# Softmax attention of two stages rebuilt: probabilities divided on GpSimd, values stationary, output born turned

## The reference

```python
# first block, for each head: the selected and the window branch
# (512 tokens: all blocks are selected and the window holds all, so both are causal softmax attention)
p_s = masked_softmax(q @ k_slc.T * scale + bias, causal)
p_w = masked_softmax(q @ k_win.T * scale + bias, causal)
y_a = (g0 * o_c + g1 * (p_s @ v_slc) + g2 * (p_w @ v_win)) @ w_up_nsa
mixed = (sigmoid(m_a) * y_a + sigmoid(m_b) * y_b) @ w_out
# second block: own and past key blocks together, causal
h_a = softmax(q_a @ k_a.T * scale, causal) @ v_a
mix = concatenate([h_m, h_a], axis=-1) @ w_out_2
```

## Time and profile before

| | us |
|---|---|
| median of 3 runs (1792.4 to 1796.67) | 1793.6 |
| span of the profiled execution (first to last instruction) | 1789.7 |
| sw, first score to the closing dummy matmuls | 284.4 to 373.0 |
| stick_breaking begins; mix_branches begins | 376.3; 457.7 |
| ma, first score to the closing dummy matmuls | 1165.0 to 1210.4 |
| out_route begins | 1212.6 |
| busy, share of the span: PE, PEld, DVE, ACT, POOL | 94%, 64%, 43%, 28%, 11% |

### The profile page before, as it was taken

The page is one execution under the profiler, slowest core; times in us unless marked ns, Lnnn a source line. Parts: engine busy times, 40 slices in busy tenths (PEclk is TensorE's granted clock), DMA queues, the critical chain, the costliest instruction groups (busy, mean ns, idle before and its releaser), DMA issues. The chain is left out here.

```text
span 1789.7 us, 21660 instructions
## 1 busy us (share of the span) xinstructions
PE 1676.2 (94%) x8246; PEld 1148.9 (64%) x8247; DVE 776.4 (43%) x1339; ACT 500.7 (28%) x821; POOL 190.5 (11%) x250
## 2 busy tenths in 40 slices
PE   6999999999999999999999999989999999999982
PEld 4788887766777878878887778778833333333321
DVE  7345224768676688423335455454621111111114
ACT  4322324546323212222224433253211011111101
POOL 1020000000112122200003000001211011110101
PEclk9999999989999999999999999999999999999996
DMA  9423220025444677422221222127799999999995
GB/s 309 116 71 118 94 94 1 1 78 180 173 153 164 215 239 246 151 71 94 94 94 36 89 76 71 48 98 300 314 378 424 423 424 424 425 424 425 424 418 210
DMA packets 114500, 366.34 MB, mean 205 GB/s; under 512 B 21723, under 2 KB 24967, under 8 KB 89807
## 3 DMA queue, kind: packets, MB, share of 16 engines
q1 hardware_dynamic: 108219, 355.45, 52.7%
q0 software_dynamic: 5760, 9.02, 1.4%
q10 hardware_dynamic: 404, 0.30, 0.1%
HBM read 359.85 MB, written 16.84 MB: 210 GB/s over the span
## 5 line engine op out<-in xcount | busy, mean ns | idle before, releaser
L2505 PE MATMUL x_upa<-x_ring,x_Ta 128*64 128x512 f32 x608 | 135.1, 593 | 12.1 <-DMA x_ring<-in_w_expert_up_dram 12.1
L2505 PE MATMUL x_gpa<-x_ring,x_Ta 128*64 128x512 f32 x608 | 135.8, 599 | 4.8 <-DMA x_ring<-in_w_expert_gate_dram 3.1
L2505 PEld LDWEIGHTS x_upa<-x_ring,x_Ta 128*64 128x64 f32 x608 | 46.6, 137 | 97.9 <-issue 97.9
L2505 PEld LDWEIGHTS x_gpa<-x_ring,x_Ta 128*64 128x64 f32 x608 | 46.2, 138 | 90.7 <-issue 88.8
L374 DVE TENSOR_TENSOR p_lo<-p_raw,p_hi 128x2048 fp32r<-128x2048 f32 (+1 forms) x20 | 44.8, 2238 | 137.0 <-ACT p_hi L687 137.0
L381 PE MATMUL fr_p<-p_hi,u_high 128*128 128x512 f32 x224 | 89.1, 398 | 0.0
L382 PE MATMUL fr_p<-p_lo,u_high 128*128 128x512 f32 x224 | 88.0, 393 | 0.0
L383 PE MATMUL fr_p<-p_hi,u_low 128*128 128x512 f32 x224 | 88.0, 393 | 0.0
L2567 ACT ACTIVATE x_siga<-x_gpa 128x512 f32<-128x512 f32 x19 | 11.3, 597 | 241.6 <-PE x_gpa L2505 241.6
L2530 PE MATMUL x_y0a<-x_ring,x_aTa 128*64 128x512 f32 x304 | 72.9, 600 | 5.1 <-ACT x_aTa L2572 4.5
L687 ACT ACTIVATE p_hi<-p_raw 128x2048 fp32r<-128x2048 f32 (+1 forms) x20 | 37.4, 1872 | 125.0 <-DMA p_raw<-in_w_in_dram 125.0
(11 more groups left out here) (886 smaller groups left out, 3979.9 us busy)
## 6 DMA issues: line engine op xcount, KB each, us to landing
x_ring<-in_w_expert_up_dram SPq DMA_DIRECT2D x64, 1024.0 KB, 28.1
x_ring<-in_w_expert_down_dram SPq DMA_DIRECT2D x64, 1024.0 KB, 27.7
x_ring<-in_w_expert_gate_dram SPq DMA_DIRECT2D x64, 1024.0 KB, 26.9
p_raw<-in_w_in_dram SPq DMA_DIRECT2D x18, 1024.0 KB, 5.1
adaw0m<-in_w_ada_dram SPq DMA_DIRECT2D x6, 2048.0 KB
adaw1m<-in_w_ada_dram SPq DMA_DIRECT2D x6, 2048.0 KB, 9.2
ada_first<-in_ada_w_dram SPq DMA_DIRECT2D x8, 1024.0 KB, 5.3
w_raw0m<-in_mlp_w_dram SPq DMA_DIRECT2D x8, 1024.0 KB, 7.2
```

The source lines that it names most:

```text
L2505: mm = nc.tensor.matmul(ps[CAP * f:CAP * f + CAP, :], self.xT[:, k, CAP * f:CAP * f + CAP], w[m + f][k // 4][:, k % 4, :], start=(k == 0), ...
```

## The change

`HeadPairs` goes, and `softmax_attention` is written anew.

- DVE inverts the sums after three tiles and again after the fourth (`invert`), and POOL multiplies each tile's probabilities in SBUF by that coefficient, and in sw by the gate too, before they are turned: 8 instructions a pair.
- `pT` now holds a whole head (four key blocks of 512 queries) and there are two, one for each head. ACT copies the second head's turned tiles, all four, and DVE the first head's. In ma they lie in the space of `heads_out`.
- `weigh` runs once a pair: the values (128x64) are stationary, the turned probabilities move (512, 384, 256 and 128 columns for key blocks 0 to 3), and the two heads go to partitions 0 to 63 and 64 to 127 of one bank. In sw the second branch accumulates on the first in PSUM, and 8 more matmuls against the identity add `B.oa`, the compressed branch.
- One DVE instruction a unit (`take`) copies the bank out, in sw with a negative step that undoes the reversed order. The output has its columns on the partitions, so the flips of `mix_branches` and half of the transposes of `out_route`, with their copies, go. The rows of `w_up_nsa` are loaded in the new order of the heads by two DMAs of 64 partitions.
- PE's list: the scores of the next pair are split around the turning of tile 3 of the first head.

```diff
+    def __init__(self, keys, values, gate=None):
+        self.keys, self.values, self.gate = keys, values, gate
...
+TURN_BANK = [0, 0, 1, 0]
+TURN_COL = [0, P, 0, 0]
...
+def softmax_attention(nc, C, tag, qT, branches, out, units=4, bias=None, shared_out=None, flipped=False, turned_at=None, ahead=None, after=None):
...
+        def turned_of(j):
+            return tps[TURN_BANK[j]][:, TURN_COL[j]:TURN_COL[j] + P * (j + 1)]
+        def copy(eng, op, p, h, j):
+            eng.wait_ge(turned, 8 * p + 4 * h + max(j, 1) + 1)
             if j == 0:
+                eng.wait_ge(weighed, p)
+            op(pT[h][:, 0:j + 1, P * j:P * j + P], turned_of(j).rearrange("p (b n) -> p b n", n=P)).then_inc(copied[h], 1)
         with nc.Block() as block:
             @block.sync
             def _(sp):
@@ -1367,80 +1283,139 @@
 
             @block.tensor
             def _(pe):
+                def scores(p, order):
+                    i, br = p // nb, branches[p % nb]
+                    for h, j in order:
+                        r = slice(64 * h, 64 * h + 64)
+                        if (h, j) == (1, 1):
+                            pe.wait_ge(shared, p + 1)
+                        mm = nc.tensor.matmul(logits_of(h, j), qT(i)[r, P * j:P * j + P], br.keys(i, h, P * (j + 1))[r, :],
+                                              start=True, stop=True)
+                        if (h, j) == (0, 1):
+                            mm.then_inc(shared, 1)
+                    if order[-1] == PAIR_ORDER[-1]:
+                        mm.then_inc(scores_ready, 1)
+                def turn(p, h, j):
+                    pe.wait_ge(scaled, 8 * p + 4 * h + j + 1)
+                    if j == 0:
+                        pe.wait_ge(copied[1 - h], 4 * (p + h))
+                    elif j == 3:
+                        pe.wait_ge(copied[h], 4 * p + 2)
+                    for b in range(j + 1):
+                        mm = nc.tensor.transpose(turned_of(j)[:, P * b:P * b + P], probs_of(h, j)[:, P * b:P * b + P], C.ident[:, :])
+                    mm.then_inc(turned, 1)
+                def weigh(p):
+                    i, k = p // nb, p % nb
+                    last = k == nb - 1
+                    for h in range(2):
+                        pe.wait_ge(copied[h], 4 * p + 4)
+                    if k == 0:
+                        pe.wait_ge(out_done, i)
+                    for b in range(NT):
+                        for h in range(2):
+                            mm = nc.tensor.matmul(ops[64 * h:64 * h + 64, P * b:TOK], branches[k].values(b, h, i), pT[h][:, b, P * b:TOK],
+                                                  start=(k == 0 and b == 0), stop=(last and not shared_out and b == NT - 1),
+                                                  skip_group_check=True)
+                    if last and shared_out:
+                        for j in range(NT):
+                            for h in range(2):
+                                mm = nc.tensor.matmul(ops[64 * h:64 * h + 64, P * j:P * j + P], shared_out(j, h, i), C.ident[:, :],
+                                                      start=False, stop=(j == NT - 1), skip_group_check=True)
+                    mm.then_inc(weighed, 1)
+                scores(0, PAIR_ORDER)
+                fill(nc, C, ops, 3)
+                for p in range(pairs):
+                    for j in range(3):
+                        turn(p, 0, j)
+                    if p + 1 < pairs:
+                        pe.wait_ge(scores_read, 8 * (p + 1))
+                        scores(p + 1, PAIR_ORDER[:4])
+                    turn(p, 0, 3)
+                    if p + 1 < pairs:
+                        scores(p + 1, PAIR_ORDER[4:])
+                    for j in range(NT):
+                        turn(p, 1, j)
+                    weigh(p)
+                fill(nc, C, sps[0], 2)
...
+                def logits(p, h, j):
                     if j == 0:
+                        if h == 0:
+                            dve.wait_ge(scores_ready, p + 1)
+                        if p:
+                            dve.wait_ge(turned, 8 * p - 4 + 4 * h)
+                    v.tensor_tensor_reduce(probs_of(h, j), logits_of(h, j), (bias(h, p // nb) if bias else C.ban)[:, P * (NT - 1 - j):512],
+                                           1.0, 3e38, ALU.add, ALU.min, low[h][:, j:j + 1]).then_inc(scores_read, 1)
+                def invert(p, h, a, b):
+                    dve.wait_ge(exps, 8 * p + 4 * h + b)
+                    v.reciprocal(coef[h][:, a:b], sums[h][:, a:b]).then_inc(coef_ready, 1)
+                def take(i):
+                    dve.wait_ge(weighed, nb * (i + 1))
+                    x = ops[:, :]
+                    if flipped:
+                        x = bass.AP(tensor=x.tensor, offset=x.offset + P - 1, ap=[x.ap[0], [P, NT], [-1, P]])
+                        v.tensor_copy(out(i).rearrange("p (t n) -> p t n", n=P), x).then_inc(out_done, 1)
+                    else:
+                        v.tensor_copy(out(i), x).then_inc(out_done, 1)
                 if bias:
                     dve.wait_ge(C.bias_in, 16)
+                for p in range(pairs):
+                    for j in range(NT):
+                        logits(p, 0, j)
+                    logits(p, 1, 0)
+                    logits(p, 1, 1)
+                    invert(p, 0, 0, 3)
+                    logits(p, 1, 2)
+                    invert(p, 0, 3, NT)
+                    logits(p, 1, 3)
+                    invert(p, 1, 0, 3)
+                    for j in range(3):
+                        copy(dve, v.tensor_copy, p, 0, j)
+                    invert(p, 1, 3, NT)
+                    copy(dve, v.tensor_copy, p, 0, 3)
+                    if p and p % nb == 0:
+                        take(p // nb - 1)
+                take(units - 1)
...
+            @block.gpsimd
+            def _(pool):
+                for p in range(pairs):
+                    gate = branches[p % nb].gate
+                    for h in range(2):
+                        for j in range(NT):
+                            pool.wait_ge(coef_ready, 4 * p + 2 * h + 1 + (j == 3))
+                            if gate:
+                                ins = pool.tensor_scalar(probs_of(h, j), probs_of(h, j), coef[h][:, j:j + 1], gate(h, p // nb)[:, j:j + 1],
+                                                         ALU.mult, ALU.mult)
+                            else:
+                                ins = pool.tensor_scalar(probs_of(h, j), probs_of(h, j), coef[h][:, j:j + 1], None, ALU.mult)
+                            ins.then_inc(scaled, 1)
...
+                def copies(p):
                     for j in range(NT):
+                        copy(act, lambda dst, src: nc.scalar.activation(dst, src, ACT.Copy), p, 1, j)
+                for p in range(pairs):
+                    if p:
+                        copies(p - 1)
+                    for h in range(2):
+                        for j in range(NT):
+                            act.wait_ge(scores_read, 8 * p + 4 * h + j + 1)
+                            nc.scalar.activation(probs_of(h, j), probs_of(h, j), ACT.Exp, scale=-1.0, bias=low[h][:, j:j + 1],
+                                                 accum_out=sums[h][:, j:j + 1]).then_inc(exps, 1)
+                copies(pairs - 1)
...
-                for k in range(4):
-                    for t in range(NT):
-                        mm = nc.tensor.matmul(tps[k][:, P * t:P * t + P], B.oa[:, t, P * k:P * k + P], C.flip[:, :],
-                                              start=True, stop=True)
-                    mm.then_inc(turned, 1)
...
-                    low(v, low_of[0][0][:, k, :], tps[k][:, :], high[0][0][:, k, :]).then_inc(heads_low, 1)
+                    low(v, low_of[0][0][:, k, :], B.oT[0][:, k, :], high[0][0][:, k, :]).then_inc(heads_low, 1)
...
-                    act.wait_ge(turned, k + 1)
-                    copy(high[0][0][:, k, :], tps[k][:, :], heads_high)
-                act.wait_ge(w_in[0], 16)
+                    copy(high[0][0][:, k, :], B.oT[0][:, k, :], heads_high)
+                act.wait_ge(w_in[0], 32)
...
+        own_heads = 4
...
-                for k in range(KD):
+                for k in range(own_heads):
                     for t in range(NT):
                         mm = nc.tensor.transpose(ps[k][:, P * t:P * t + P], cat(t, k), C.ident[:, :])
                     mm.then_inc(turned, 1)
...
-                        for b, n in enumerate(("w_up_nsa", "w_up_sb")):
-                            sp.dma_start(wu[b][:, :, :], A[n][0].rearrange("(k p) n -> p k n", p=P)).then_inc(w_in[b], 16)
+                        for half in range(2):
+                            sp.dma_start(wu[0][64 * half:64 * half + 64, :, :],
+                                         A["w_up_nsa"][0, 256 * half:256 * half + 256, :].rearrange("(k d) n -> d k n", d=HD)).then_inc(w_in[0], 16)
```

(12 more changed lines are left out.)

234 lines of the change are left out of this document (42 added, 192 removed).

## The result

Nine runs of the changed kernel on the chip have a median of 1807.46 us (1803.98 to 1811.18), nine of the kernel before 1795.86. The ratio is 1.0065, 95% interval 1.0048 to 1.0082: slower by 11.6 us, where 1780.5 and a gain were forecast. The profiled execution spans 1808.9 us. The stages, from first matmul to first matmul, read from the timeline, in brackets the time with TensorE at half clock. Mixing counts from its first product, so the 16 flips stand in the row of stick_breaking where there are any.

The account below looks back on a forecast made before the run. PE and its short waits were taken to bound sw and ma, 134.0 us. New pairs of 9.35 us gave 79.6 + 41.3 = 120.9, a gain of 13.1: 1776.6 profiled, plus 3.9 makes 1780.5 us; range 1770 to 1801.

Parts of the forecast that it names:

- S: POOL's scaling of a whole pair's eight tiles: 5.6 us, between 4.8 by select and 6.4 by two inputs.
- The second rival: POOL becomes the bound, deciding from S = 7.2 on; with S = 7.8 the kernel takes 1801 us; chance 0.11.
- The long ring: Chain through ACT, DVE, POOL and PE from one pair to the next: 7.45 us plus POOL's three tiles, 9.15.
- steps 1 to 11: The long ring's parts in order, from three exponentials to ACT's copy of 512 columns: 9.15 us in all.
- steps 5 and 7: The next pair's first four scores, 1.53 us; DVE's copy of 512, 0.74, with the other four scores, 0.83, beside it.
- step 4: Hand-over and PE's turning of three blocks of tile 2 on the long ring: 0.38 us.
- step 9: ACT's copies of 128 and 256 columns of the second head, with hand-over, on the long ring: 0.6 us.
- T: Time of one pair in sw and ma: 9.35 us, the long ring's 9.15 plus 0.2 for matmul mode changes.
- The third rival: TensorE's clock falls in both stages; at half clock for half the time, 15 us slower, 1809; chance 0.12.
- 8T + 4.8: Length of sw, its pairs plus the stage's ends: 79.6 us.
- 4T + 3.9: Length of ma, its pairs plus the ends, with -1.5 for the last pair's missing four scores: 41.3 us.
- the ring through POOL: Shorter ring in both stages, through POOL's whole pair: 3.04 + S, 8.6 us a pair.

Follow-up runs that it names:

- the first experiment: The changed kernel with a second scalar, a column of ones, in POOL's scaling instruction in ma: 1794.02 us, ratio 0.9984.
- 3: The changed kernel with the gate left out of sw's scaling, so that POOL's instruction there has one scalar too: 1825.66 us in one run.
- 8: The changed kernel with 14 POOL instructions of 128x512 in different scalar forms added behind ma's last pair: 1817.71 us in one run.
- the fifth experiment: The fourth experiment's kernel with the compressed branch's records ahead of the second branch's weighing and the bank's copy behind the next pair's last logits: 1792.53 us, ratio 0.9975.
- the fourth experiment: The first experiment's kernel with dummy matmuls of 128 columns in PE's waits: 1793.61 us, ratio 0.9971.
- 10: The ninth's kernel with the next pair's first four scores reordered, PE waiting for the eighth logits only ahead of the fourth score: 1787.18 us, ratio 0.9947.
- 11: The kernel of 10 with the next pair's last two scores moved behind the second head's turning of tile 2: 1787.17 us, ratio 0.9961.
- the ninth: The fifth experiment's kernel with DVE scaling only tile 2 of the first head and POOL the other seven tiles: 1786.79 us, ratio 0.9947.
- 6: The fifth experiment's kernel with DVE scaling the first head's first three tiles and POOL the other five: 1791.14 us, ratio 0.9967.
- experiment 12: The changed kernel with the fourth experiment's dummy matmuls, POOL's one-scalar form left in ma: 1805.82 us, ratio 1.0043.
- experiment 7: The kernel before, run unchanged for a second profile: 1793.08 us in one run.

## Why the prediction was wrong

**The step that failed** is POOL's price: "The new instruction has one tensor and one or two scalars from memory, so I take the middle of select and two inputs: S = 5.6". One value was taken for two forms. sw's is at the lower bound (4.75), ma's above the upper one (8.5 for 7.8), and I had let the count of inputs speak for the price. The second rival gave the mechanism, S above 7.2, and its formula holds: 3.04 + 8.5 = 11.54 for pairs of 11.62. Its time, 1801, was for both stages at 7.8. Experiments 1, 3 and 8 show the price from three sides. The first takes 8.1 us out of ma, 5.4 of it by the distance of its pairs, 9.82 in place of 11.62 three times.

The profile's span is 32.3 us over the 1776.6 forecast. ma is 13.0 over its 41.3 (8.1 the price, 2.4 the clock, the rest the steps below), sw 7.4 over its 79.6, the mixing stage 0.2, `out_route` 1.4, and some 10 lie in code that is as before.

- *The long ring in sw.* POOL's three tiles took 1.67 with the hand-over, as taken. The round shown is 0.68 over the 9.15 of steps 1 to 11. The two pieces of scores (steps 5 and 7) make 0.4 of it: eight in a row took 2.36, in two pieces they take 1.71 + 1.06 = 2.77. The sum had 0.2 for all changes between half and full rows. "TensorEngine Tiling", Key Properties, in the Trainium skill, by which each change drains the array, would have had 0.2 more and was nearer; the two pieces, 0.2 us each over their share of the unbroken run, agree with it in kind. Tile 2's turning (step 4) and ACT's first copies (step 9) were 0.1 each over. At the seam of two units `B.oa` and the bank's copy make the pair 10.16 where 9.69 stands between; T was 9.95 on the mean where 9.35 was forecast. On the ring itself that is 10.02 and 9.82, as the fifth experiment shows.
- *Weighing* takes 2.2 us as worked out, so the halves run together.
- *The clock.* The third rival had 0.50 for half of the time of both stages; it was 21 of 141 us. It struck the last pair of either stage, 2.3 us in sw and 2.4 in ma by the fourth experiment; an earlier fall in ma (1198.4 to 1201.9) left its pair at 11.62. The last weighing of ma takes 4.07 us where 2.2 was forecast:

```profile
1222.13 1.09 PE L1318 MATMUL opsma<-pT0ma,va 128*64 128x512 f32 x1 [0.73 <-issue]
...
1226.20 1.98 PE L147 MATMUL sps0ma<-ban,ident 128*128 128x512 f32 x4
```

- *The stage's ends.* 8T + 4.8 gives 84.4 for T = 9.95, and 2.3 of clock 86.7, for 87.0 measured. In ma 4T + 3.9 gives 50.4 for T = 11.62, and 54.3 were measured. The clock's 2.4 are part of that, and the -1.5 for step 5 doesn't belong there: the ring through POOL has no step 5 to leave out.
- *Mixing stage and out_route.* Right: from SP's first instruction of the mixing stage to the next stage's first matmul it was 64.0 us and is 64.2; the first product of `out_route` comes 3.7 behind its start for 3.8. In place of flips and transposes PE waits:

```profile
460.83 0.53 PE L381 MATMUL mx<-wu_high,oT_high 128*128 128x512 f32 x1 [3.04 <-DVE oT_low L374]
```

```profile
1232.24 0.47 PE L381 MATMUL dp0o<-w_hi0o,ah0o 128*128 128x512 f32 x1 [1.82 <-DVE al0o L2176]
```

- *"All later stages start by as much earlier"* took their length for fixed. Of the 19.2 us between the two spans ma, sw and mixing account for 7.7 (9.0 - 1.5 + 0.2) and `out_route` for 1.4, with 3 us more at half clock; 10.1 lie in code that is as before. The medians are 11.6 apart, 7.7 of it shown by those three stages. Runs of the kernel before differ in the granted clock too, 0.985 in one of 1792.84 us and 0.977 in one of 1800.25; its median was 0.980, 0.972 for the changed kernel, 0.978 for experiments 1, 4 and 5. Why the unchanged stages of the changed kernels tend to more time at half clock (`out_route` 10 us in place of 7 in most, 7 in experiments 10 and 11, which then took 84.0) stays open: no run tells a shift of the stages in time from chance.

Had the price been that of the select in both stages, the forecast gain of 13 would still have been 3 us, as in the first experiment; clock, seam and tile 2 together make it 9. In the rows of sw and ma alone, 139.5 us before, it is 0.6 less in the first experiment, 5.3 in the fourth and 9.1 in the ninth; the other 2 us of the first experiment's gain are of the size by which profiles of one program differ elsewhere.

## What to carry to other kernels

Price a new instruction by its form, not by its count of inputs: where no row shows the form, time it alone first, since one missing operand was worth 13 us here. When a change ties engines into a ring, write down every ring, the one through the buffers' release (`scores_read`) too: shortening one uncovered the next (experiments 6 and 9 to 11). Measure a ring's round at an instruction that stands on it. A stage whose PE waits between short turnings may lose its clock; dummy matmuls in waits that exist anyway kept it in sw and, with POOL quick, in ma, but not in ma with POOL slow (experiment 12).

## What the runs showed of the hardware

- POOL's `tensor_scalar` on 128x512 float32 takes 1.49 to 1.56 us with one operation and 0.62 to 0.77 with two; 128 columns 0.60 and 0.45 (scalars from memory). DVE's with two scalars takes 0.48 for 384 columns.
- A split of one run of half-row matmuls into two, with full-row turnings between, costs 0.4 us (2.77 for 2.36).
- Two profiles of one program differ by 4.0 us up to sw, with 14 us at half clock there for 3 (experiment 7).
- While PE was at half clock, the last weighing took 4.0 to 4.1 us in place of 2.2.
